# Compression products over columns ordered block by block, with the keys' low parts in two banks of their own

## The chip, the cores and the metric

One Trainium2 chip, one core. The metric is the device time of one execution in microseconds (us); of the runs shown the median is taken. TensorE does the matrix products, VectorE, ScalarE and GpSimd the elementwise work, SyncE issues most transfers.

## What is computed

One step of a decoder layer (D_MODEL 2048) for 256 prompt tokens and 8 samples of 8 tokens, 320 tokens in all. An input projection feeds three attention branches; their outputs are gated, projected, merged and added to the input. The change touches one part of it, the compressed keys and values of the first branch, for the 9 sequences (8 samples with 256 cached rows each, and the prompt):

```python
def compress_tokens(kv, phi_pos, phi_w1, phi_w2):
    # block i covers rows [i*16, i*16 + 32); phi = 2-layer MLP, separate weights for k and v
    sub = kv[:, :n_half * 16].reshape(b, n_half, 16, 2, 2, 128)
    pos = phi_pos.reshape(2, 2, 16, 128)
    w1 = phi_w1.reshape(2, 2, 16, 128, 128)
    for m in range(2):
        part = einsum('bnscgd,csdh->bncgh', sub + pos[:, m], w1[:, m])
        part = part[:, m:m + n_cmp]
        hid = part if hid is None else hid + part
    out = einsum('bncgh,che->bncge', silu(hid), phi_w2)
```

With 256 rows a sequence has 16 half blocks of 16 rows and 15 compressed blocks. Two groups of heads by 9 sequences give 18 row sets, so 288 half blocks, plus two columns for the position embedding.

## The kernel before, in words

**Products.** All weights come as tiles of 2048 x 128, in one stream of 144 tiles that alternate between two buffers u = 0 and 1. A tile is loaded into `raw[u]`, ScalarE rounds it to float32r in `w_hi[u]` (`split_hi`, L536), VectorE puts the rest into `w_lo[u]` (`split_lo`, L814), and TensorE makes three products for each of 16 blocks: high x high, high x low, low x high (`part`, L1327 to L1329), over 320 columns. A split for buffer u waits until TensorE has finished the tile before in it (`mm_done[u]`), and TensorE starts a tile when `lo_ready[u]` says that its low part is there. So while TensorE works on one buffer's tile, the other buffer is split. The next load of a buffer waits for `lo_ready[u]`. The order of the instructions on each engine is written out by hand.

**The compression stage.** At tile pairs J_PHI to J_PHI+3 buffer 0 holds query weights (a `part` of 320 columns) and buffer 1 the compression weights: k = 0, 1 for the keys (c = 0) and k = 2, 3 for the values (c = 1), each with m = 0 (first half of a block) and m = 1 (second half). The raw rows lie in `cmp_t`, by row set q, page g, position s in a half block and half block n within the page (8 per page); the last row set is the position embedding. `cmp_high` (ScalarE, L643) rounds them into `c_hi`, whose row for position s holds 290 columns that count: 16 for each of the 18 row sets and then 2 for the position embedding. `cmp_low` (VectorE, L985) subtracts: for the keys into `c_lo`, in place of the raw rows and in their order, and for the values into `c_lo_pos`, in the order of `c_hi`. The keys are split in two calls by sequences (long before their use), the values in two calls by positions (s below 8, then the rest). The values' high part may overwrite that of the keys only when TensorE has used it: `c_half` comes after the eighth position of k = 1, and the second half waits behind the split of the next weight tile.

For each position TensorE then makes three products (L1450, L1452 or L1454, L1455), all into one bank: S0 and P0 for the keys, S1 and P1 for the values. For the keys the second product reads `c_lo` by a strided pattern of 37 runs of 8 columns, 296 in all; the others read 290 columns in one piece. `pe.wait_ge(c_lo_rdy, ...)` stands before the first position, and for the values before the ninth too.

**Behind it.** `hidden_in` (VectorE, L1000 to L1003) adds the position column of each half and the two halves shifted by one block: four instructions, each of which waits for the one before (`ch.link`). ScalarE's tanh (L658), two more instructions of VectorE (`hidden_out`) and a product with `w_phi2` follow. For the keys this stands in VectorE's order at k = 2, for the values at k = 3. S2 and OB were used last for the rows of the memory values, which ScalarE copies out (L632, `v_rows_rdy`) before the stage; S2 is written again by the product that follows `hidden_out` (L1460).

Of the kernel before, what the change touches and what calls it, by code (L numbers as in the profile page):

```python
# [24 lines left out]
PAGES = PAST // PAGE  # L25
KEYS_S = PAST + DEC_SEQ
SEQS = DEC_BATCH + 1
# [7 lines left out]
NGP = 32  # L35
FIRST_SEQS = 5
HALF = TOK // 2
OUT_PARTS = ((0, 0, 2), (0, 2, 6), (0, 6, 8), (0, 8, 12), (0, 12, 16), (1, 0, 4), (1, 4, 8), (1, 8, 12), (1, 12, 14), (1, 14, 16))
HEAD = ((0, 2), (2, 4), (4, 8), (8, 12), (12, 16))

f32 = mybir.dt.float32
f32r = mybir.dt.float32r
i32 = mybir.dt.int32
ALU = mybir.AluOpType
ACT = mybir.ActivationFunctionType
# [33 lines left out]
def build(nc, A):  # L79
    ctx = ExitStack()  # L80
    with ctx:
# [20 lines left out]
        w_hi = fixed("w_hi", [P, 2, KB, P], f32r)  # L102
        w_lo = fixed("w_lo", [P, 2, KB, P], f32r)
# [15 lines left out]
        st = fixed("st", [P, 16])  # L119
# [21 lines left out]
        cmp_t = at("cmp_t", [P, 2, 2 * SEQS + 1, SEQ], f32, Z_)  # L141
# [132 lines left out]
        def raw_blocks(c, q0, q1, half):  # L274
            return cmp_t[:, c, q0:q1, :].rearrange("p q (g s n) -> p (q g) s n", g=PAGES, s=CMP_STRIDE)[:, :, positions(half), :]

        def by_position(t, q0, q1, half):
            return t[:, positions(half), q0 * CMP_STRIDE:q1 * CMP_STRIDE].rearrange("p s (q n) -> p q s n", n=PAGE // CMP_STRIDE)

        def low_blocks(c, q0, q1, half):  # L280
            if c == 1:
                return by_position(c_lo_pos, q0, q1, half)
            return c_lo[:, q0:q1, :].rearrange("p q (g s n) -> p (q g) s n", g=PAGES, s=CMP_STRIDE)

        def high_blocks(q0, q1, half):
            return by_position(c_hi, q0, q1, half)

        def cross_rows(i, q):

# [241 lines left out]
        def _(act):  # L531
# [106 lines left out]
                for u in range(2):  # L638
                    split_hi(u, k + (J_CMP + 1))

            def cmp_high(c, q0, q1, half=None):
                src, dst = raw_blocks(c, q0, q1, half), high_blocks(q0, q1, half)
                nc.scalar.activation(dst, src, ACT.Copy).then_inc(c_hi_rdy, 1)  # L643

            act.wait_ge(cmp_in, 16 * PAGES * 2 * FIRST_SEQS)
            cmp_high(0, 0, 2 * FIRST_SEQS)
# [5 lines left out]
            cmp_high(0, 2 * FIRST_SEQS, 2 * SEQS + 1)  # L652
            split_hi(0, J_PHI)
            split_hi(1, J_PHI)

# [5 lines left out]
            split_hi(1, J_PHI + 1)  # L661
            split_hi(0, J_PHI + 2)
            act.wait_ge(c_half, 1)
            cmp_high(1, 0, 2 * SEQS + 1, 0)
            split_hi(1, J_PHI + 2)
            cmp_high(1, 0, 2 * SEQS + 1, 1)
            split_hi(0, J_PHI + 3)
            hidden_tanh(0)
            split_hi(1, J_PHI + 3)
# [138 lines left out]
        def _(dve):  # L808
            ch = Chain(dve, dve_chain)
# [122 lines left out]
            v, y, t = st[:, 8:10], st[:, 10:12], st[:, 12:14]  # L932
# [33 lines left out]
            for k in range(2):  # L966
                for u in range(2):
# [3 lines left out]
                    rows = kv_t[:, 2 * k + u, 0:SEQ].rearrange("p (g n s) -> p g s n", g=PAGES, s=CMP_STRIDE)  # L971
# [10 lines left out]
            def cmp_low(c, q0, q1, count, half=None):  # L982
                src, high, dst = raw_blocks(c, q0, q1, half), high_blocks(q0, q1, half), low_blocks(c, q0, q1, half)
                dve.wait_ge(c_hi_rdy, count)
                nc.vector.tensor_tensor(dst, src, high.bitcast(f32), ALU.subtract).then_inc(c_lo_rdy, 1)  # L985

            with dve.Fori(0, J_PHI - J_Q - 2) as k:
                for u in range(2):
                    query_tile(u, k + J_Q, one(q_t, k * 2 + u))
            cmp_low(0, 0, 2 * FIRST_SEQS, 1)  # L990
            for u in range(2):
                query_tile(u, J_PHI - 2, q_t[:, 8 + u, :])
            cmp_low(0, 2 * FIRST_SEQS, 2 * SEQS + 1, 2)
            for u in range(2):
                query_tile(u, J_PHI - 1, q_t[:, 10 + u, :])

            def hidden_in(c):
                first, second = ((S0, P0), (S1, P1))[c]
                rows = hx[:, c, 0:270].rearrange("p (q n) -> p q n", n=N_CMP)
                ch.link(nc.vector.tensor_copy(st[:, c:c + 1], first[:, 288:289]))  # L1000
                ch.link(nc.vector.tensor_scalar_add(rows, first[:, 0:288].rearrange("p (q n) -> p q n", n=CMP_STRIDE)[:, :, 0:N_CMP], st[:, c:c + 1]))
                ch.link(nc.vector.tensor_copy(st[:, c:c + 1], second[:, 289:290]))
                nc.vector.scalar_tensor_tensor(rows, second[:, 0:288].rearrange("p (q n) -> p q n", n=CMP_STRIDE)[:, :, 1:CMP_STRIDE],  # L1003
                                               st[:, c:c + 1], rows, ALU.add, ALU.add).then_inc(hid_x, 1)

            def hidden_out(c):
                dve.wait_ge(hid_e, c + 1)
# [3 lines left out]
            for k in range(4):  # L1011
                query_tile(0, J_PHI + k, q_t[:, 12 + k, :])
                if k == 2:
                    hidden_in(0)
                    hidden_out(0)
                dve.wait_ge(mm_done[1], J_PHI + k + 2)
                dve.sem_inc(w_free[1], 1)
                if k == 1:
                    cmp_low(1, 0, 2 * SEQS + 1, 3, 0)
                if k < 3:  # L1020
                    split_lo(1, J_PHI + k + 1)
                if k == 1:
                    cmp_low(1, 0, 2 * SEQS + 1, 4, 1)
                if k == 3:
                    hidden_in(1)
                    hidden_out(1)
# [232 lines left out]
            v, y, t = st[:, 0:2], st[:, 3:5], st[:, 6:8]  # L1259
# [55 lines left out]
        def _(pe):  # L1315
# [85 lines left out]
            for m, first in enumerate((0, P, TOK - P)):  # L1401
                mm = nc.tensor.matmul(P0[:, m * P:m * P + NGP], v_tmp[:, 0, first:first + P], fold[:], start=True, stop=True)
# [16 lines left out]
            for t in range(4):  # L1419
                u, j = t % 2, J_MEM + 2 + t // 2  # L1420
                pe.wait_ge(lo_ready[u], j + 2)
                for i in range(4):
                    kb = 4 * t + i
                    high, low = (w[:, u, 4 * i:4 * i + 4, :].rearrange("p k c -> p (k c)") for w in (w_hi, w_lo))
                    for n in range(2):
                        out, rows = (S2, OB)[n], slice(n * P, (n + 1) * P)
                        nc.tensor.matmul(out[:], m_hi[:, kb, rows], high, start=(kb == 0), stop=False)  # L1427
                        nc.tensor.matmul(out[:], m_lo[:, kb, rows], high, start=False, stop=False)  # L1428
                        mm = nc.tensor.matmul(out[:], m_hi[:, kb, rows], low, start=False, stop=(kb == KB - 1))  # L1429
# [5 lines left out]
                for u in range(2):  # L1435
                    part(u, k + J_Q, h_hi, h_lo, TOK, ALL)

            used = 2 * SEQS * CMP_STRIDE + CMP_LEN // CMP_STRIDE
            n = PAGE // CMP_STRIDE
            runs = -(-used // n)  # L1440
# [263 lines left out]
            for n, first in enumerate(firsts):  # L1704
                mm = nc.tensor.matmul(S0[:, n:n + 1], y_sum[:, 0, first:first + P], ones[:, 0:1], start=True, stop=True, skip_group_check=True)
# [124 lines left out]
```

## Time and profile before

| | |
|---|---|
| Median of 3 runs | 1113.35 us (1113.16 to 1113.83) |
| Profiled execution, span from first to last instruction | 1110.9 us |
| Median above that span | 2.45 us |
| TensorE busy | 1100.0 us (99%), 8020 products |
| VectorE, ScalarE, GpSimd busy | 606.3, 419.5, 66.8 us |
| Mean granted TensorE clock | 0.996 |

The profiled execution's own time is not listed apart from its span. Products are pipelined: the duration of one reaches beyond the start of the next, so what a product costs is the distance between starts. The third column of a timeline row names the engine, then come the line, the operation, what is written and read, and its shape (partitions x columns); at the end stands how long the engine had been idle and who released it.

### The profile page before, as it was taken

The page shows a single profiled execution, that of the slowest core. Times are in us where ns is not written, and L with a number is a line of the kernel's source. Part 1 is how long each engine was busy: PE and PEld are TensorE (multiplying, and loading weights), DVE is VectorE, ACT ScalarE, POOL GpSimd, SP SyncE. Part 2 cuts the span into 40 slices and gives each one's busy share as a digit, 9 for nine tenths or more (in the row PEclk, how much of TensorE's full clock was granted, in tenths as well). Part 3 has the DMA queues.
Part 4 walks back from the last instruction along what each step waited for, and adds up shares of the span by engine and source line. Part 5 has one row for each costly group of instructions (what it writes and reads, how often), then busy time and mean ns, then how long its engine had stood idle before and what let it go on. Part 6 is the DMA issues. An engine that isn't in the chain of part 4 may idle for free.

```text
span 1110.9 us, 19312 instructions
## 1 busy us (share of the span) xinstructions
PE 1100.0 (99%) x8020; PEld 1077.8 (97%) x8020; DVE 606.3 (55%) x884; ACT 419.5 (38%) x566; POOL 66.8 (6%) x121
## 2 busy tenths in 40 slices
PE   9999999999999999999999999999999999999996
PEld 7998999999999999999999999999999999999996
DVE  6794443536456667664454467455455454454445
ACT  6733322424335444443333344333333333333332
POOL 0014000000000000001100000000000000002220
PEclk9999999999999999999999999999999999999998
DMA  8556685544444232358888744544544444464342
GB/s 297 196 189 201 228 279 189 179 152 152 168 147 173 83 113 110 114 171 295 288 277 306 257 149 171 171 171 171 171 167 153 168 145 144 147 242 146 148 150 95
DMA packets 64081, 202.03 MB, mean 182 GB/s; under 512 B 6647, under 2 KB 35607, under 8 KB 45831
## 3 DMA queue, kind: packets, MB, share of 16 engines
q1 hardware_dynamic: 58888, 185.68, 48.8%
q0 software_dynamic: 2400, 10.89, 2.8%
q10 hardware_dynamic: 2718, 4.41, 1.1%
q8 instruction: 55, 0.90, 0.3%
q14 instruction: 20, 0.16, 0.0%
HBM read 193.61 MB, written 11.53 MB: 185 GB/s over the span
## 4 chain that ended last, share of the span: by engine, by line
PE 99%; DVE 1%; issue 0%; DVEq 0%
PE bank L1327 27%; PE bank L1328 27%; PE bank L1329 27%; PE bank L1679 1%; PE bank L1360 1%; PE bank L1455 1%; PE bank L1450 1%; PE bank L1429 1%; PE bank L1428 1%; PE bank L1427 1%; PE bank L1594 1%; PE bank L1517 0%; PE bank L1452 0%; PE bank L1685 0%; PE bank L1345 0%; PE bank L1454 0%
## 5 line engine op out<-in xcount | busy, mean ns | idle before, releaser
L536 ACT ACTIVATE w_hi<-raw 128x2048 fp32r<-128x2048 f32 x140 | 268.1, 1915 | 572.2 <-PE bank L1329 479.9
L1327 PE MATMUL bank<-h_hi,w_hi 128*128 128x320 f32 x1536 | 479.7, 312 | 0.0
L1329 PE MATMUL bank<-h_hi,w_lo 128*128 128x320 f32 x1536 | 474.6, 309 | 0.0
L1328 PE MATMUL bank<-h_lo,w_hi 128*128 128x320 f32 x1536 | 474.5, 309 | 0.0
L814 DVE TENSOR_TENSOR w_lo<-raw,w_hi 128x2048 fp32r<-128x2048 f32 x140 | 325.2, 2323 | 186.4 <-ACT w_hi L536 186.2
L1327 PEld LDWEIGHTS bank<-h_hi,w_hi 128*128 128x128 f32 x1536 | 288.4, 188 | 3.9 <-issue 3.5
L1328 PEld LDWEIGHTS bank<-h_lo,w_hi 128*128 128x128 f32 x1536 | 288.5, 188 | 0.4
L1329 PEld LDWEIGHTS bank<-h_hi,w_lo 128*128 128x128 f32 x1536 | 288.4, 188 | 0.0
L1328 PE MATMUL bank<-oz_lo,w_hi 128*128 128x320 f32 x256 | 78.9, 308 | 0.0
L1329 PE MATMUL bank<-oz_hi,w_lo 128*128 128x320 f32 x256 | 78.8, 308 | 0.0
L1327 PE MATMUL bank<-oz_hi,w_hi 128*128 128x320 f32 x256 | 78.8, 308 | 0.0
L1327 PE MATMUL bank<-mrg_both,w_hi 128*128 128x320 f32 x224 | 69.0, 308 | 0.0
L1328 PE MATMUL bank<-mrg_both,w_hi 128*128 128x320 f32 x224 | 69.0, 308 | 0.0
L1329 PE MATMUL bank<-mrg_both,w_lo 128*128 128x320 f32 x224 | 69.0, 308 | 0.0
L1201 DVE TENSOR_TENSOR g<-bank,inv 128x320 f32<-128x320 f32 x32 | 15.7, 491 | 72.2 <-PE bank L1329 72.2
L1327 PEld LDWEIGHTS bank<-oz_hi,w_hi 128*128 128x128 f32 x256 | 48.1, 188 | 0.0
L1328 PEld LDWEIGHTS bank<-oz_lo,w_hi 128*128 128x128 f32 x256 | 48.1, 188 | 0.0
L1329 PEld LDWEIGHTS bank<-oz_hi,w_lo 128*128 128x128 f32 x256 | 48.1, 188 | 0.0
L1327 PEld LDWEIGHTS bank<-mrg_both,w_hi 128*128 128x128 f32 x224 | 42.0, 188 | 0.0
L1328 PEld LDWEIGHTS bank<-mrg_both,w_hi 128*128 128x128 f32 x224 | 42.0, 188 | 0.0
L1329 PEld LDWEIGHTS bank<-mrg_both,w_lo 128*128 128x128 f32 x224 | 42.0, 188 | 0.0
L1211 DVE SCALAR_TENSOR_TENSOR bt<-g_t,bank 128x320 f32<-128x320 f32 x16 | 7.8, 487 | 37.8 <-PE bank L1329 37.8
(347 smaller groups left out, 1127.5 us busy)
## 6 DMA issues: line engine op xcount, KB each, us to landing
raw<-in_stream SPq DMA_DIRECT2D x140, 1024.0 KB, 5.0
cmp_t<-in_cmp_pages SPq DMA_DIRECT2D x32, 128.0 KB, 4.2
kt_moba<-in_moba_k SPq DMA_DIRECT2D x16, 256.0 KB, 3.6
kt_mem<-in_mem_k SPq DMA_DIRECT2D x8, 512.0 KB, 6.3
vs_moba<-in_moba_v SPq DMA_DIRECT2D x16, 256.0 KB
vs_mem<-in_mem_v SPq DMA_DIRECT2D x8, 512.0 KB
out_win_old<-in_cache_win POOLq DMA_DIRECT2D x8, 512.0 KB, 3.7
raw<-in_stream SPq DMA_DIRECT2D x10, 256.0 KB, 9.9
```

The costliest lines, as they stand in the source:

```text
L536: nc.scalar.activation(w_hi[:, u], raw[:, u], ACT.Copy).then_inc(hi_ready[u], 1)
L814: nc.vector.tensor_tensor(w_lo[:, u], raw[:, u], w_hi[:, u].bitcast(f32), ALU.subtract).then_inc(lo_ready[u], 1)
L1201: nc.vector.tensor_tensor(g12[:, u, br, :], W[u][:, 0:TOK], inv[:], ALU.mult).then_inc(w_free[u], 1)
L1327: nc.tensor.matmul(out[:, 0:n], w_hi[:, u, kb, :], hi[:, kb, :], start=(kb == first), stop=False)
L1328: nc.tensor.matmul(out[:, 0:n], w_hi[:, u, kb, :], lo[:, kb, :], start=False, stop=False)
L1329: mm = nc.tensor.matmul(out[:, 0:n], w_lo[:, u, kb, :], hi[:, kb, :], start=False, stop=(kb == last))
L1360: mm = nc.tensor.matmul(W[0][:, 0:TOK], raw_a[:, kb, :], x_t[:, kb, :], start=(kb == 0), stop=(kb == KB - 1))
L1427: nc.tensor.matmul(out[:], m_hi[:, kb, rows], high, start=(kb == 0), stop=False)
L1428: nc.tensor.matmul(out[:], m_lo[:, kb, rows], high, start=False, stop=False)
L1429: mm = nc.tensor.matmul(out[:], m_hi[:, kb, rows], low, start=False, stop=(kb == KB - 1))
L1450: nc.tensor.matmul(out[:, 0:used], w_hi[:, 1, s, :], c_hi[:, s, 0:used], start=(s == 0), stop=False, skip_group_check=True)
L1455: mm = nc.tensor.matmul(out[:, 0:used], w_lo[:, 1, s, :], c_hi[:, s, 0:used], start=False, stop=(s == CMP_STRIDE - 1), skip_group_check=True)
```

## The change

The columns of `c_hi` and of `c_lo_pos` are ordered by half block first and row set second: two columns for the position embedding (first half), 16 groups of 18 row sets, two columns for the position embedding again (second half), 292 in all. The first half (m = 0) then needs columns 0 to 271 and the second half columns 20 to 291: 272 each, since the last half block of a row set is not used by the first half, nor the first by the second. ScalarE and VectorE copy and subtract page by page (two instructions in place of one), reading 8 neighbouring half blocks and writing them 18 columns (72 bytes) apart, and do the position columns in small instructions. `c_lo` keeps its order; its products can no longer be added in the same bank, so they go to S2 (m = 0) and OB (m = 1), and `hidden_in` adds those for the keys with four more instructions. TensorE waits once more, for S2 and OB to be copied out, before the stage.

```diff
+CMP_USED = 2 * SEQS * CMP_STRIDE + CMP_LEN // CMP_STRIDE
+CMP_COLS = 2 * SEQS * N_CMP + CMP_LEN // CMP_STRIDE
...
+        def block_columns(t, q0, q1, half, g):
+            columns = t[:, positions(half), 2:2 + CMP_STRIDE * 2 * SEQS].rearrange("p s (g n q) -> p g q s n", g=PAGES, q=2 * SEQS)
+            return columns[:, g, q0:q1]
+
+        def raw_pos(c, half):
+            return cmp_t[:, c, 2 * SEQS, 0:PAGE].rearrange("p (s n) -> p s n", s=CMP_STRIDE)[:, positions(half), 0:2]
+
+        def pos_columns(t, half, m):
+            return t[:, positions(half), m * CMP_USED:m * CMP_USED + 2]
...
-            def cmp_high(c, q0, q1, half=None):
-                src, dst = raw_blocks(c, q0, q1, half), high_blocks(q0, q1, half)
-                nc.scalar.activation(dst, src, ACT.Copy).then_inc(c_hi_rdy, 1)
+            def cmp_high(c, q0, q1, half=None, pos=True):
+                if pos:
+                    for m in range(2):
+                        nc.scalar.activation(pos_columns(c_hi, half, m), raw_pos(c, half), ACT.Copy)
+                nc.scalar.activation(block_columns(c_hi, q0, q1, half, 0), raw_blocks(c, q0, q1, half, 0), ACT.Copy)
+                nc.scalar.activation(block_columns(c_hi, q0, q1, half, 1), raw_blocks(c, q0, q1, half, 1), ACT.Copy).then_inc(c_hi_rdy, 1)
...
+            def cmp_low(c, q0, q1, count, half=None, pos=True):
                 dve.wait_ge(c_hi_rdy, count)
-                nc.vector.tensor_tensor(dst, src, high.bitcast(f32), ALU.subtract).then_inc(c_lo_rdy, 1)
+                if pos:
+                    for m in range(2 if c else 1):
+                        nc.vector.tensor_tensor(low_pos(c, half, m), raw_pos(c, half), pos_columns(c_hi, half, m).bitcast(f32), ALU.subtract)
+                    if c == 0:
+                        rest = [t[:, 2 * SEQS, 0:PAGE].rearrange("p (s n) -> p s n", s=CMP_STRIDE)[:, :, 2:] for t in (c_lo, cmp_t[:, 0])]
+                        nc.vector.tensor_copy(*rest)
+                for g in range(PAGES):
+                    src, high, dst = raw_blocks(c, q0, q1, half, g), block_columns(c_hi, q0, q1, half, g), low_blocks(c, q0, q1, half, g)
+                    ins = nc.vector.tensor_tensor(dst, src, high.bitcast(f32), ALU.subtract)
+                ins.then_inc(c_lo_rdy, 1)
...
-                ch.link(nc.vector.tensor_copy(st[:, c:c + 1], first[:, 288:289]))
...
+                ch.link(nc.vector.tensor_copy(st[:, c:c + 1], first[:, 0:1]))
+                ch.link(nc.vector.tensor_scalar_add(rows, by_row(first, 2), st[:, c:c + 1]))
+                ch.link(nc.vector.tensor_copy(st[:, c:c + 1], second[:, 271:272]))
+                ins = nc.vector.scalar_tensor_tensor(rows, by_row(second, 0), st[:, c:c + 1], rows, ALU.add, ALU.add)
+                if c == 0:
+                    for m, low in enumerate((S2, OB)):
+                        ch.link(ins)
+                        ch.link(nc.vector.tensor_copy(st[:, c:c + 1], low[:, 288 + m:289 + m]))
+                        blocks = low[:, 0:288].rearrange("p (q n) -> p q n", n=CMP_STRIDE)[:, :, m:m + N_CMP]
+                        ins = nc.vector.scalar_tensor_tensor(rows, blocks, st[:, c:c + 1], rows, ALU.add, ALU.add)
...
+            pe.wait_ge(v_rows_rdy, 2 + 4)
...
+                columns = slice(0, CMP_COLS) if m == 0 else slice(2 * SEQS + 2, 2 * SEQS + 2 + CMP_COLS)
...
-                    nc.tensor.matmul(out[:, 0:used], w_hi[:, 1, s, :], c_hi[:, s, 0:used], start=(s == 0), stop=False, skip_group_check=True)
+                    nc.tensor.matmul(out[:, 0:CMP_COLS], w_hi[:, 1, s, :], c_hi[:, s, columns], start=(s == 0), stop=False)
                     if c == 0:
-                        nc.tensor.matmul(out[:, 0:runs * n].rearrange("p (q n) -> p q n", n=n), w_hi[:, 1, s, :], low[:, s, 0:runs], start=False, stop=False, skip_group_check=True)
+                        nc.tensor.matmul((S2, OB)[m][:, 0:runs * n].rearrange("p (q n) -> p q n", n=n), w_hi[:, 1, s, :], low[:, s, 0:runs],
+                                         start=(s == 0), stop=(s == CMP_STRIDE - 1))
                     else:
-                        nc.tensor.matmul(out[:, 0:used], w_hi[:, 1, s, :], c_lo_pos[:, s, 0:used], start=False, stop=False, skip_group_check=True)
-                    mm = nc.tensor.matmul(out[:, 0:used], w_lo[:, 1, s, :], c_hi[:, s, 0:used], start=False, stop=(s == CMP_STRIDE - 1), skip_group_check=True)
+                        nc.tensor.matmul(out[:, 0:CMP_COLS], w_hi[:, 1, s, :], c_lo_pos[:, s, columns], start=False, stop=False)
+                    mm = nc.tensor.matmul(out[:, 0:CMP_COLS], w_lo[:, 1, s, :], c_hi[:, s, columns], start=False, stop=(s == CMP_STRIDE - 1))
```

## Rows read from the trace of the kernel before

**Rows 1.** The chain that ended last: shares of the span by engine.

```profile
PE 99%; DVE 1%; issue 0%; DVEq 0%
```

**Rows 2.** Waits of TensorE: total us, times, longest us.

```profile
PE bank L1345 <- DVE ones L822: 1.7, 1, 1.7
PE bank L1693 <- DVE y_diag L1274: 1.6, 1, 1.6
PE bank L1717 <- DVE y_last L1257: 0.7, 1, 0.7
```

**Rows 3.** Compression products by form; busy times by engine, then granted clock (1.00), DMA.

```profile
L1455 PE MATMUL bank<-c_hi,w_lo 128*128 128x290 f32 x64 | 19.2, 299 | 0.0
L1450 PE MATMUL bank<-c_hi,w_hi 128*128 128x290 f32 x64 | 19.0, 297 | 0.0
L1452 PE MATMUL bank<-c_lo,w_hi 128*128 128x296 f32 x32 | 10.3, 323 | 0.0
L1454 PE MATMUL bank<-c_lo_pos,w_hi 128*128 128x290 f32 x32 | 9.5, 298 | 0.0
...
274.30:280.70 6.40, 6.40 (x50) 6.40 (x49) 2.78 (x2) 1.92 (x1) 0.00 (x0) 1.00 0.46 127
```

**Rows 4.** Timeline of TensorE, first products of tiles: start us, us, engine, line.

```profile
225.99 0.31 PE L1327 MATMUL bank<-h_hi,w_hi 128*128 128x320 f32 x1
...
233.03 0.30 PE L1450 MATMUL bank<-c_hi,w_hi 128*128 128x290 f32 x1
...
239.92 0.31 PE L1327 MATMUL bank<-h_hi,w_hi 128*128 128x320 f32 x1
...
260.87 0.29 PE L1450 MATMUL bank<-c_hi,w_hi 128*128 128x290 f32 x1
...
274.35 0.29 PE L1450 MATMUL bank<-c_hi,w_hi 128*128 128x290 f32 x1
...
280.80 0.62 PE L1460 MATMUL bank<-hid,w_phi 128*128 128x270 f32 x2
```

**Rows 5.** Timeline of TensorE in the memory stage: 256 columns, then 512.

```profile
69.95 0.28 PE L1327 MATMUL bank<-m_hi,w_hi 128*128 128x256 f32 x1
...
91.38 0.39 PE L1427 MATMUL bank<-w_hi,m_hi 128*128 128x512 f32 x1
...
102.13 0.39 PE L1429 MATMUL bank<-w_lo,m_hi 128*128 128x512 f32 x1
102.36 0.39 PE L1427 MATMUL bank<-w_hi,m_hi 128*128 128x512 f32 x1
```

**Rows 6.** Timeline of VectorE around the compression.

```profile
202.27 2.83 DVE L985 TENSOR_TENSOR c_lo<-cmp_t,c_hi 128x2560 fp32r<-128x2560 f32 x1
...
217.41 2.56 DVE L985 TENSOR_TENSOR c_lo<-cmp_t,c_hi 128x2304 fp32r<-128x2304 f32 x1 [1.00 <-ACT c_hi L643]
...
254.15 2.69 DVE L985 TENSOR_TENSOR c_lo_pos<-cmp_t,c_hi 128x2432 fp32r<-128x2432 f32 x1 [2.69 <-PE bank L1455]
...
258.95 2.68 DVE L985 TENSOR_TENSOR c_lo_pos<-cmp_t,c_hi 128x2432 fp32r<-128x2432 f32 x1
...
266.00 0.16 DVE L1002 COPY st<-bank 128x1 f32<-128x1 f32 x1
266.20 0.50 DVE L1003 SCALAR_TENSOR_TENSOR hx<-bank,st,hx 128x270 f32<-128x270 f32 x1
...
269.52 2.29 DVE L814 TENSOR_TENSOR w_lo<-raw,w_hi 128x2048 fp32r<-128x2048 f32 x1 [1.55 <-ACT w_hi L536]
```

**Rows 7.** Timeline of ScalarE around the compression.

```profile
250.57 2.25 ACT L643 ACTIVATE c_hi<-cmp_t 128x2432 fp32r<-128x2432 f32 x1 [1.45 <-PE bank L1455]
...
266.74 0.43 ACT L658 ACTIVATE he<-hx 128x270 f32<-128x270 f32 x1 [3.69 <-DVE hx L1003]
267.58 1.92 ACT L536 ACTIVATE w_hi<-raw 128x2048 fp32r<-128x2048 f32 x1 [0.41 <-PE bank L1455]
```

**Rows 8.** VectorE's copy of the prompt's rows (L972): ns min/median/max, first and last start.

```profile
L972 DVE COPY cmp_t<-kv_t x4: 392/400/403, 121.2 to 142.3; 128x256 f32<-128x256 f32 x4
```

More of the change, by code:

```diff
@@ L272, in positions, with raw_blocks, low_blocks, low_pos @@
             return slice(0, CMP_STRIDE) if half is None else slice(half * CMP_STRIDE // 2, (half + 1) * CMP_STRIDE // 2)
[L274 to L280, printed above, removed]
-            if c == 1:
[L282 to L286, printed above, removed]
+        def raw_blocks(c, q0, q1, half, g):
+            return cmp_t[:, c, q0:q1, :].rearrange("p q (g s n) -> p g q s n", g=PAGES, s=CMP_STRIDE)[:, g, :, positions(half), :]
+        def block_columns(t, q0, q1, half, g):
[5 more added lines that the diff above has]
+            return t[:, positions(half), m * CMP_USED:m * CMP_USED + 2]
+        def low_blocks(c, q0, q1, half, g):
+            if c == 1:
+                return block_columns(c_lo_pos, q0, q1, half, g)
+            return c_lo[:, q0:q1, :].rearrange("p q (g s n) -> p g q s n", g=PAGES, s=CMP_STRIDE)[:, g]
+        def low_pos(c, half, m):
+            if c == 1:
+                return pos_columns(c_lo_pos, half, m)
+            return c_lo[:, 2 * SEQS, 0:PAGE].rearrange("p (s n) -> p s n", s=CMP_STRIDE)[:, :, 0:2]
         def cross_rows(i, q):
@@ L639, in _ @@
                     split_hi(u, k + (J_CMP + 1))
-            def cmp_high(c, q0, q1, half=None):
-                src, dst = raw_blocks(c, q0, q1, half), high_blocks(q0, q1, half)
-                nc.scalar.activation(dst, src, ACT.Copy).then_inc(c_hi_rdy, 1)
+            def cmp_high(c, q0, q1, half=None, pos=True):
[4 more added lines that the diff above has]
+                nc.scalar.activation(block_columns(c_hi, q0, q1, half, 1), raw_blocks(c, q0, q1, half, 1), ACT.Copy).then_inc(c_hi_rdy, 1)
             act.wait_ge(cmp_in, 16 * PAGES * 2 * FIRST_SEQS)
-            cmp_high(0, 0, 2 * FIRST_SEQS)
+            cmp_high(0, 0, 2 * FIRST_SEQS, pos=False)
             for u in range(2):
@@ L651, in _ @@
             act.wait_ge(pos_in, 16)
-            cmp_high(0, 2 * FIRST_SEQS, 2 * SEQS + 1)
+            cmp_high(0, 2 * FIRST_SEQS, 2 * SEQS)
             split_hi(0, J_PHI)
@@ L663, in _ @@
             act.wait_ge(c_half, 1)
-            cmp_high(1, 0, 2 * SEQS + 1, 0)
+            cmp_high(1, 0, 2 * SEQS, 0)
             split_hi(1, J_PHI + 2)
-            cmp_high(1, 0, 2 * SEQS + 1, 1)
+            cmp_high(1, 0, 2 * SEQS, 1)
             split_hi(0, J_PHI + 3)
@@ L980, in query_tile @@
                 split_lo(u, j + 1)
-            def cmp_low(c, q0, q1, count, half=None):
-                src, high, dst = raw_blocks(c, q0, q1, half), high_blocks(q0, q1, half), low_blocks(c, q0, q1, half)
+            def cmp_low(c, q0, q1, count, half=None, pos=True):
                 dve.wait_ge(c_hi_rdy, count)
-                nc.vector.tensor_tensor(dst, src, high.bitcast(f32), ALU.subtract).then_inc(c_lo_rdy, 1)
+                if pos:
[8 more added lines that the diff above has]
+                ins.then_inc(c_lo_rdy, 1)
             with dve.Fori(0, J_PHI - J_Q - 2) as k:
@@ L989, in _ @@
                     query_tile(u, k + J_Q, one(q_t, k * 2 + u))
-            cmp_low(0, 0, 2 * FIRST_SEQS, 1)
+            cmp_low(0, 0, 2 * FIRST_SEQS, 1, pos=False)
             for u in range(2):
                 query_tile(u, J_PHI - 2, q_t[:, 8 + u, :])
-            cmp_low(0, 2 * FIRST_SEQS, 2 * SEQS + 1, 2)
+            cmp_low(0, 2 * FIRST_SEQS, 2 * SEQS, 2)
             for u in range(2):
@@ L999, in hidden_in, with by_row @@
                 rows = hx[:, c, 0:270].rearrange("p (q n) -> p q n", n=N_CMP)
-                ch.link(nc.vector.tensor_copy(st[:, c:c + 1], first[:, 288:289]))
[L1001 to L1004, printed above, removed]
+                def by_row(bk, first):
+                    return bk[:, first:first + 270].rearrange("p (n q) -> p q n", q=2 * SEQS)
+                ch.link(nc.vector.tensor_copy(st[:, c:c + 1], first[:, 0:1]))
[8 more added lines that the diff above has]
+                        ins = nc.vector.scalar_tensor_tensor(rows, blocks, st[:, c:c + 1], rows, ALU.add, ALU.add)
+                ins.then_inc(hid_x, 1)
             def hidden_out(c):
@@ L1018, in _ @@
                 if k == 1:
-                    cmp_low(1, 0, 2 * SEQS + 1, 3, 0)
+                    cmp_low(1, 0, 2 * SEQS, 3, 0)
                 if k < 3:
@@ L1022, in _ @@
                 if k == 1:
-                    cmp_low(1, 0, 2 * SEQS + 1, 4, 1)
+                    cmp_low(1, 0, 2 * SEQS, 4, 1)
                 if k == 3:
@@ L1436, in _ @@
                     part(u, k + J_Q, h_hi, h_lo, TOK, ALL)
-            used = 2 * SEQS * CMP_STRIDE + CMP_LEN // CMP_STRIDE
             n = PAGE // CMP_STRIDE
-            runs = -(-used // n)
+            runs = -(-CMP_USED // n)
+            pe.wait_ge(v_rows_rdy, 2 + 4)
             low = c_lo[:].rearrange("p q (g s n) -> p s (q g) n", g=PAGES, s=CMP_STRIDE)
```

## The prediction

> **What bounds the kernel now.** I read the chain of waits first. It lies on TensorE for 99% of the span [rows 1], so only what TensorE does or waits for can move the time. Next, who TensorE waited for: three waits, 4.0 us together, one on the first instruction and two in the final normalization [rows 2]. Between them it never stood still for another engine, so a product that becomes shorter makes the end earlier by as much, and work added to VectorE or ScalarE costs nothing until it makes a TensorE tile late.
>
> Then the products that the diff touches [rows 3]: 64 + 64 + 32 = 160 of 290 columns, and 32 of 296 columns (low parts of the keys). The durations there (297 to 323 ns) are no price: they overlap. The price is the distance from start to start, read in the timeline.
> - 320 columns: 48 products from 225.99 to 233.03, 7.04 us, 146.7 ns each [rows 4].
> - 290 columns: the last compression tile, 48 products from 274.35 to 280.80, 6.45 us, 134.4 ns each [rows 4].
> - Tile with the strided low product: 233.03 to 239.92, 6.89 us [rows 4]. It is 0.44 us longer than the one above for the same number of products, so each of its 16 products of 296 columns costs about 27 ns more than a product of 290.
> - 256 columns: the product at 69.95 is the fourth of 192, so 189 of them reach to 91.38: 113.4 ns each [rows 5].
> - 512 columns: 48 products from 91.38 to 102.36, 228.8 ns each [rows 5].
>
> The granted clock is 1.00 of 2.4 GHz there [rows 3], so streaming alone would take 133.3, 120.8, 106.7 and 213.3 ns for 320, 290, 256 and 512 columns. What lies above streaming is 13.4, 13.6, 6.7 and 15.5 ns.
>
> **The change, part by part.**
> 1. *160 products go from 290 to 272 columns.* No row shows 272. From the 290 row, with the slope between 290 and 320 (12.3 ns over 30 columns, 0.41 ns a column), it is 134.4 - 18 x 0.41 = 127.0 ns: 7.4 ns less, times 160 is 1.18 us. The line between 256 and 290 (0.62 ns a column) gives 123.3 ns, 1.8 us in all. If 272 carried only the 6.7 ns above streaming that 256 does, it would be 120.0 ns, 2.3 us in all. I take 1.2 us, since three of four widths carry 13 to 16 ns above streaming and 272 lies above 256; 2.3 us stays as the far end.
> 2. *Second halves read from column 20* (80 bytes into a row) instead of column 0: 80 of the 160 products. No row isolates a start offset. The nearest is the strided low product, 27 ns dearer; its short runs are a far stronger disturbance than one offset. The bounds are 0 and 80 x 27 ns = 2.2 us; I take 0, since the stream itself stays contiguous.
> 3. *Low parts of the keys into two other banks.* The 32 products keep their 296 columns and their strided read, so their price stays. TensorE now changes banks before and after each. The nearest rows are the value products of the memory, which change bank after every third: from the last product in one bank (102.13) to the first in the other (102.36) is 0.23 us, the mean of all of them [rows 5]. I take 0. The extra 27 ns might also vanish with the shared bank: 32 x 27 = 0.9 us, the bound on the gain's side. The one added wait, for the memory rows to have left those banks, stands on copies that ScalarE makes before the queries' tiles even begin: 0.
> 4. *ScalarE's splits.* Each of the four high-part instructions becomes two, and three of the four calls get two tiny ones for the position columns. Elements go from 2432 to 2304 + 32 for the value halves. Between 270 elements in 0.43 us and 2432 in 2.25 us lie 0.84 ns an element and 0.20 us of fixed time [rows 7], so three more instructions less 96 elements make +0.5 us per call. The high part of the first value half ends at 252.82; VectorE takes it up at 254.15 [rows 6, 7]. Hidden by 1.3 us, by 0.8 us after the addition.
> 5. *VectorE's splits.* A tiny copy takes 0.16 us [rows 6]. A value half gets two tiny instructions and the fixed time of one more, and loses 96 elements (0.1 us): +0.4 us at most. The binding point is the second value half: it runs from 258.95 for 2.68 us, to 261.63 [rows 6], and TensorE wants it 24 products into its tile, at 260.87 + 24 x 0.134 = 264.1 [rows 4]. Margin 2.5 us, less 24 x 7.4 ns because the tile now runs faster, less 0.8 us for both halves: 1.5 us remain. Cost 0. The key splits are further from their use.
> 6. *The key sum gets four more instructions* in a chain where each waits for the one before: two copies (0.16 us) and two additions over 270 columns (0.50 us), with 0.04 us between [rows 6]: +1.5 us. ScalarE's tanh, which started at 266.74 and took 0.43 us [rows 7], waits for that; queued behind it on ScalarE is the weight split that started at 267.58 and fed VectorE's at 269.52 [rows 6, 7]. Now the tanh ends at 268.7, the weight split (1.9 us) at 270.6, and VectorE's (2.29 us) at 272.9. TensorE wants it when its next 320-column tile ends, at 274.35 [rows 4], 0.36 us earlier after the shorter tile: 274.0. Margin 1.1 us: cost 0, though this is the thinnest cover. The value sum has no added instruction.
> 7. *Reads and writes with a step of 72 bytes* in the ScalarE and VectorE splits, and from the sum's banks. What the trace has is a VectorE copy with a step of 64 bytes on its reading side: 256 elements in 400 ns [rows 8], about 1.04 ns an element after some 0.13 us of fixed time. The present low-part subtraction runs at that rate too (2.69 us for 2432 elements, [rows 6]). So a long step on a read did not go below one element a cycle. No row has a long step on a write. Bounds: 0, or twice the time per element. I take 0.
>
> The Trainium skill ("SBUF — State Buffer", section "Door 1: The DMA port swizzle") speaks against part 7: it says that memory is served in lines of 16 bytes, and that each access that crosses to a new line pays. By it the splits would slow down and the sum would be that of the slower rival below. The copy in the trace does not bear it out for reads by VectorE.
>
> **Sum:** -1.18 us, nothing added. The profiled execution's span goes from 1110.9 to 1109.7 us; the median of 1113.35 us lies 2.45 us above that span, taken as unchanged, and goes to 1112.2; I say 1112.1.
>
> **The rivals.**
> - *Cheaper spacing* (chance 0.18). Products of 272 behave like those of 256, or the low products lose their extra cost. The times are 1113.35 - 2.3 = 1111.05, or 1113.35 - 1.2 - 0.9 = 1111.25, both together 1110.15. For it: the 256 rows do have the smaller excess. Against it: 290, 320 and 512 agree on the larger one, and the strided read stays.
> - *The gain is not kept* (chance 0.10). The offset of part 2, or the bank changes, take 5 to 15 ns from a product here and there: between 1112.6 and 1114.3, most likely about 1113.3. Against it: no row shows such a loss for a contiguous stream.
> - *Slower: long steps double the time per element* (chance 0.07). VectorE first: its two value halves take 5.2 us each. The first ends at 259.35, the weight split behind it at 261.6 instead of before 260.87 (0.7 us of standstill), the second half at 266.8 where TensorE is at 264.65 (2.15 us), and the late key sum adds 0.3 us to the next tile. That is 3.2 - 1.2 = +2.0 us, 1115.35. If ScalarE's writes double too (2.2 us more per call), the value halves start 0.75 us later, and the key splits that began on VectorE at 202.27 and 217.41 [rows 6] push the weight splits behind them past TensorE's tile starts by 1.0 and 1.7 us: 1118.8. It decides from where the second half's margin is used up: 1.5 us over 4608 elements, 0.33 ns each, about 1.3 times the present time per element.
> - Main case, chance 0.65.
>
> **How the numbers follow.** A measurement of this kernel can tell about 0.2%, 2.2 us, from no change. The main case (1.2 us) lies inside, and so does "not kept". Of the cheaper-spacing rival about 0.14 passes 2.2 us. The slower rival is counted whole (0.07), though its milder form comes out just inside, and 0.01 is added for other losses. Faster 0.14, same 0.78, slower 0.08. The range reaches down to 1110.8 (cheaper spacing without both effects together) and up to 1113.9 (most of "not kept"); outside are the slower rival and the two extremes.
>
> **What would show it.** Right: spacing of about 127 ns in the value tiles, so 6.1 us for 48 products instead of 6.45; 6.65 us instead of 6.89 in the key tiles; still no wait of TensorE between the first and the last stage; splits of ScalarE and VectorE at 0.83 and 1.04 ns an element. Wrong: 5.8 us for a value tile (cheaper spacing); a TensorE wait on the low parts of the values or on a weight split near 260 or 274 us (slower rival, or the thin cover of part 6); second-half tiles longer than first-half tiles (the offset).

## The result and the profile after

The change made the kernel slower: 1118.76 us median (1118.10 to 1121.70, 5 runs) against 1113.18 us (1112.59 to 1113.83) beside it, a ratio of 1.0056 (95% interval 1.0045 to 1.0067). The forecast was 1112.1 us, in a range from 1110.8 to 1113.9, with 0.08 for slower. Of the experiments' executions two ran at a mean granted clock of 0.85 and 0.87 (1193.6 us for the narrower products alone, 1179.0 us for the step in the keys' splits alone); they count in no ratio, and without them the two medians given below as 1111.84 and 1116.59 us would be 1111.70 and 1116.53 us.

The page of the changed kernel, its first line and the chain of waits by engine, where [rows 1] had 99% on TensorE:

```profile
span 1119.9 us, 19336 instructions
...
PE 94%; DVE 3%; ACT 1%; DMA 1%; issue 0%; SPq 0%; DVEq 0%; ACTq 0%
```

VectorE, ScalarE and a transfer are now on the chain. The waits of TensorE (total us, times, longest) have three lines that [rows 2] did not have:

```profile
PE bank L1359 <- DVE w_lo L828: 3.5, 2, 2.8
...
PE bank L1483 <- DVE w_lo L828: 1.4, 1, 1.4
PE bank L1483 <- DVE c_lo_pos L1006: 1.2, 1, 1.2
```

TensorE's timeline shows where they are: the last product ahead of each standstill and the first two behind it.

```profile
212.47 0.31 PE L1361 MATMUL bank<-h_hi,w_lo 128*128 128x320 f32 x1
213.45 0.41 PE L1359 MATMUL bank<-h_hi,w_hi 128*128 128x320 f32 x1 [0.67 <-DVE w_lo L828]
213.70 0.30 PE L1360 MATMUL bank<-h_lo,w_hi 128*128 128x320 f32 x1
...
227.48 0.31 PE L1361 MATMUL bank<-h_hi,w_lo 128*128 128x320 f32 x1
230.58 0.61 PE L1359 MATMUL bank<-h_hi,w_hi 128*128 128x320 f32 x1 [2.79 <-DVE w_lo L828]
230.99 0.47 PE L1360 MATMUL bank<-h_lo,w_hi 128*128 128x320 f32 x1
...
267.47 0.31 PE L1361 MATMUL bank<-h_hi,w_lo 128*128 128x320 f32 x1
269.19 0.39 PE L1483 MATMUL bank<-c_hi,w_hi 128*128 128x272 f32 x1 [1.41 <-DVE w_lo L828]
269.42 0.28 PE L1488 MATMUL bank<-c_lo_pos,w_hi 128*128 128x272 f32 x1
...
272.19 0.29 PE L1489 MATMUL bank<-c_hi,w_lo 128*128 128x272 f32 x1
273.71 0.39 PE L1483 MATMUL bank<-c_hi,w_hi 128*128 128x272 f32 x1 [1.23 <-DVE c_lo_pos L1006]
273.94 0.28 PE L1488 MATMUL bank<-c_lo_pos,w_hi 128*128 128x272 f32 x1
```

From the first to the third row of each group, less the distances that the two products would have had anyway (147 ns for 320 columns, 125 ns for 272, 267 ns for 320 at half clock), the standstills cost 0.94, 3.10, 1.68 and 1.50 us, 7.2 us together: two before query tiles behind the keys' splits, two in the first value tile. The granted clock (the column behind the POOL busy time) fell to half, 1.2 GHz, shortly before the second one ended, and stayed there behind it, in this execution:

```profile
228.00:230.00 2.00, 0.00 (x0) 0.00 (x0) 2.00 (x2) 1.79 (x1) 0.00 (x0) 0.94 0.00 0
230.00:232.00 2.00, 1.42 (x5) 1.45 (x6) 2.00 (x3) 0.00 (x0) 0.00 (x0) 0.50 0.18 25
232.00:234.00 2.00, 2.00 (x9) 2.00 (x9) 1.08 (x1) 0.00 (x0) 0.00 (x0) 0.50 0.86 356
...
236.00:238.00 2.00, 2.00 (x13) 2.00 (x13) 0.00 (x0) 0.00 (x0) 0.00 (x0) 0.86 0.69 291
```

In it 22 products of 320 columns started 267 ns apart instead of 147: 2.6 us. The last value tile gives the other side, the gain:

```profile
283.87 0.29 PE L1483 MATMUL bank<-c_hi,w_hi 128*128 128x272 f32 x1
...
289.86 0.62 PE L1494 MATMUL bank<-hid,w_phi 128*128 128x270 f32 x2
```

48 products in 5.99 us, 124.8 ns each, where [rows 4] had 134.4. For 160 products that is 1.5 us. The account of this execution: 7.2 + 2.6 - 1.5 = +8.3 us in the stage, against +9.0 us in the span; the stage began some 0.7 us later too. This was the longest of the five executions (mean clock 0.994; the two shortest, at 0.997, took 1118.1 and 1118.2 us).

Why VectorE was late, in its own timeline, against [rows 6] (a row that ends in x2 is two instructions one after the other, with their common time):

```profile
205.67 5.05 DVE L1006 TENSOR_TENSOR c_lo<-cmp_t,c_hi 128x1280 fp32r<-128x1280 f32 x2 [2.63 <-ACT c_hi L657]
...
223.85 4.03 DVE L1006 TENSOR_TENSOR c_lo<-cmp_t,c_hi 128x1024 fp32r<-128x1024 f32 x2
...
262.36 4.58 DVE L1006 TENSOR_TENSOR c_lo_pos<-cmp_t,c_hi 128x1152 fp32r<-128x1152 f32 x2
...
269.19 4.46 DVE L1006 TENSOR_TENSOR c_lo_pos<-cmp_t,c_hi 128x1152 fp32r<-128x1152 f32 x2
```

The subtractions of a value half now take 4.5 us for 2304 elements, where 2432 had taken 2.69. ScalarE's copies grew alike: two of 1152 elements in 2.33 and 2.35 us, where one of 2432 had taken 2.25 [rows 7].

### The profile page after: what moved, and what is told of

It is laid out like the page before. It is cut to its first block, busy times and chain, and to the rows that moved or that the text cites. A ratio compares the mean times of both kernels' runs of the same rounds, so it can differ in the third digit from the quotient of the medians.

```text
span 1119.9 us, 19336 instructions
## 1 busy us (share of the span) xinstructions
PE 1102.5 (98%) x8020; PEld 1079.1 (96%) x8020; DVE 615.2 (55%) x898; ACT 428.5 (38%) x576; POOL 66.4 (6%) x121
## 4 chain that ended last, share of the span: by engine, by line
PE 94%; DVE 3%; ACT 1%; DMA 1%; issue 0%; SPq 0%; DVEq 0%; ACTq 0%
PE bank L1359 26%; PE bank L1361 26%; PE bank L1360 26%; PE bank L1713 1%; DVE c_lo L1006 1%; DVE c_lo_pos L1006 1%; PE bank L1392 1%; PE bank L1461 1%; PE bank L1460 1%; PE bank L1459 1%; ACT c_hi L657 1%; DVE w_lo L828 1%; DMA x_t<-in_x_t 1%; PE bank L1628 1%; PE bank L1483 1%; PE bank L1489 1%
```

## The experiments

**Is it the step, or the number of instructions?** The rival to the step was the additional instructions and the longer key sum. The edit puts the 8 half blocks of a page next to each other again and leaves everything else as in the change:

```diff
-            columns = ...rearrange("p s (g n q) -> p g q s n", g=PAGES, q=2 * SEQS)
+            columns = ...rearrange("p s (g q n) -> p g q s n", g=PAGES, q=2 * SEQS)
```

> The changed kernel with one thing undone: in the rows of c_hi and c_lo_pos the 8 half blocks of a row set stand next to each other again (step 4 bytes instead of 72); the number of instructions, elements, products and columns is that of the change. It leaves out the right assignment of columns to blocks. Theory 'long steps double the time per element': the halves of the values' splits go back to about 1.15 us on ScalarE and 1.35 us on VectorE, no wait of TensorE in the stage, 1113.2 - 1.5 = 1111.7 us. Rival 'two instructions and the position columns make the engines late': they stay long, about 1118.8 us.

Measured: 1111.74 us against 1113.37 (0.9986, 0.9976 to 0.9995). No wait of TensorE in the stage is left. Two groups, busy us and mean ns, of this run:

```profile
L1006 DVE TENSOR_TENSOR c_lo_pos<-cmp_t,c_hi 128x1152 fp32r<-128x1152 f32 x4 | 5.2, 1352 | 0.0
...
L656 ACT ACTIVATE c_hi<-cmp_t 128x1152 fp32r<-128x1152 f32 x2 | 2.5, 1227 | 0.0
```

The step alone makes the difference between 1111.7 and 1118.8 us. The additional instructions and the longer sum cost nothing that can be measured: the next run has neither and takes 1111.84 us.

**What are the narrower products worth?**

```diff
-    nc.tensor.matmul(out[:, 0:used], w_hi[:, 1, s, :], c_hi[:, s, 0:used], ...)
+    nc.tensor.matmul(out[:, 0:272], w_hi[:, 1, s, :], c_hi[:, s, cols], ...)   # cols = 0:272 or 20:292, three products
```

> The kernel before, with only the 160 products at 272 columns (first halves from column 0, second halves from column 20), the splits and the sum as before. It leaves out columns that the sum needs. What the narrower products are worth alone: the trace of the changed kernel has 125.0 ns from start to start for 272 columns against 134.4 for 290, so 160 x 9.4 = 1.5 us: 1111.7 us. Rival, that part of the gain in the key tiles (0.35 and 0.28 us there) comes from the banks: less than 1.5 us, about 1.3.

Measured: 1111.84 us (0.9986, 0.9976 to 0.9996), 1.5 us less. The first key tile, with all three products in one bank:

```profile
234.30 0.29 PE L1451 MATMUL bank<-c_hi,w_hi 128*128 128x272 f32 x1
...
240.84 0.31 PE L1327 MATMUL bank<-h_hi,w_hi 128*128 128x320 f32 x1
```

It takes 6.54 us. In the changed kernel, with banks of their own for the low parts, the same tile takes 6.54 us too:

```profile
240.40 0.29 PE L1483 MATMUL bank<-c_hi,w_hi 128*128 128x272 f32 x1
...
246.94 0.31 PE L1359 MATMUL bank<-h_hi,w_hi 128*128 128x320 f32 x1
```

The second key tile takes 6.60 us in both. So the banks neither cost nor save anything, and the low product keeps what it costs above the others. The gain in the key tiles is smaller because only two of their three products got narrower.

**What does a step cost by itself?** Subtractions and copies behind the last work, for example with 18 elements:

```diff
+    ch.link(nc.vector.tensor_tensor(fl[:, 2304:3456].rearrange("p (n q) -> p q n", q=18), <contiguous>, <contiguous>, ALU.subtract))
+    ach.link(nc.scalar.activation(fa[:, 2304:3456].rearrange("p (n q) -> p q n", q=18), <contiguous>, ACT.Copy))
```

> The kernel before with 20 instructions of 1152 elements added behind its last work, on memory nobody uses any more: VectorE subtractions and ScalarE copies, in which the written or the read operand has a step of 1, 2, 4, 8 or 18 elements. Theory 'each step beyond some size costs on every operand': contiguous 1.35 us (VectorE) and 1.16 us (ScalarE), with a written step of 18 about 2.35 and 2.3 us, with a read step of 18 the same. Rival 'only writes pay': a read step leaves 1.35 and 1.16 us. Rival 'it is contention between the two engines and the transfers in that stage, not the step': all of them near 1.35 and 1.16 us here, where the chip is quiet.

Lines of that run (ns, smallest, median, largest of one). VectorE: contiguous, written step 2, 4, 18, read step 18; ScalarE: contiguous, written step 2, 4, 18, read step 18:

```profile
L1328 DVE TENSOR_TENSOR raw<-raw x1: 1348/1348/1348, 1107.6 to 1107.6; 128x1152 f32<-128x1152 f32 x1
L1329 DVE TENSOR_TENSOR raw<-raw x1: 1359/1359/1359, 1109.0 to 1109.0; 128x1152 f32<-128x1152 f32 x1
L1330 DVE TENSOR_TENSOR raw<-raw x1: 2201/2201/2201, 1110.4 to 1110.4; 128x1152 f32<-128x1152 f32 x1
...
L1332 DVE TENSOR_TENSOR raw<-raw x1: 2320/2320/2320, 1114.9 to 1114.9; 128x1152 f32<-128x1152 f32 x1
...
L1336 DVE TENSOR_TENSOR raw<-raw x1: 2314/2314/2314, 1123.1 to 1123.1; 128x1152 f32<-128x1152 f32 x1
L809 ACT ACTIVATE raw<-raw x1: 1162/1162/1162, 1127.9 to 1127.9; 128x1152 f32<-128x1152 f32 x1
L810 ACT ACTIVATE raw<-raw x1: 1231/1231/1231, 1129.1 to 1129.1; 128x1152 f32<-128x1152 f32 x1
L811 ACT ACTIVATE raw<-raw x1: 2223/2223/2223, 1130.3 to 1130.3; 128x1152 f32<-128x1152 f32 x1
...
L813 ACT ACTIVATE raw<-raw x1: 2362/2362/2362, 1134.9 to 1134.9; 128x1152 f32<-128x1152 f32 x1
...
L817 ACT ACTIVATE raw<-raw x1: 2362/2362/2362, 1143.1 to 1143.1; 128x1152 f32<-128x1152 f32 x1
```

A step of 8 bytes is nearly free; one of 16 bytes and more adds 0.74 to 0.84 ns an element to VectorE's subtraction and 0.9 to 1.0 to ScalarE's copy. It makes no difference whether it stands on the reading or on the writing side, and a second operand with a step adds nothing (written and read with a step of 18: 2321 ns). No other engine works there, and the transfer engines' busy share is 0.12 during VectorE's instructions and 0.00 during ScalarE's, so contention is not the cause: that rival falls, and so does "only writes pay".

**Why did the copy of [rows 8] look free?**

```diff
+    ch.link(nc.vector.tensor_copy(fl[:, 2304:2560].rearrange("p (q n) -> p q n", q=16), fl[:, 0:256].rearrange("p (n q) -> p q n", q=16)))
```

> The kernel before with more VectorE instructions behind its last work: copies of 1152 elements with a read step of 1, 2, 3, 4, 16, 18 and a written step of 2, 3, 18; subtractions with a step of 3 and 6; additions of 504 elements from a bank with a step of 1, 2, 18; the copy of 256 elements with a step of 1 and 16. It asks why the copy in rows 8 looked free of charge. Theory: a contiguous copy runs at two elements a cycle (about 0.75 us for 1152), so that its 1.04 ns an element with a long step was already the slow form: the 256 elements take about 0.27 us contiguous and 0.4 us with a step of 16. Rival: a copy's reads are free, contiguous 0.4 us too. Step 3 (12 bytes) lies between steps 2 and 4 if each touched line of 16 bytes costs. Reads from a bank cost nothing for a step (the sum's instructions took 0.50 us in both kernels).

Copies of 1152 elements contiguous and with a step of 4; additions of 504 elements from a bank, contiguous and with a step of 18; the copy of 256 elements contiguous and with a step of 16:

```profile
L1314 DVE COPY raw<-raw x1: 750/750/750, 1108.0 to 1108.0; 128x1152 f32<-128x1152 f32 x1
...
L1317 DVE COPY raw<-raw x1: 1185/1185/1185, 1111.3 to 1111.3; 128x1152 f32<-128x1152 f32 x1
...
L1327 DVE TENSOR_SCALAR raw<-bank,ones x1: 741/741/741, 1126.7 to 1126.7; 128x504 f32<-128x504 f32 x1
...
L1329 DVE TENSOR_SCALAR raw<-bank,ones x1: 744/744/744, 1128.2 to 1128.2; 128x504 f32<-128x504 f32 x1
L1330 DVE COPY raw<-raw x1: 294/294/294, 1129.0 to 1129.0; 128x256 f32<-128x256 f32 x1
L1331 DVE COPY raw<-raw x1: 375/375/375, 1129.3 to 1129.3; 128x256 f32<-128x256 f32 x1
```

A contiguous copy runs at 0.51 ns an element ((750 - 294) / 896 elements), twice as fast as a subtraction. The copy of the kernel before was already slowed by its step; it only looked like full speed beside instructions of another kind. Reads from a bank pay nothing for a step of 8 or 72 bytes. For the subtraction a step of 12 bytes lies between (written with a step of 3 it took 1701 ns). For VectorE's copy two things do not follow the pattern of the subtraction. A step of 16 bytes and more adds less, 0.33 to 0.43 ns an element (1130 to 1243 ns with steps of 4, 16 and 18, in place of 750). And a step of 3 costs more than one of 4: 1680 ns read and 1670 written. Why is open.

**Can the step be moved to the raw rows?** The loop order inside the splits is turned, so that the row sets run innermost (for `c_lo` too; the indices are turned with it):

```diff
-    raw:     "p q (g s n) -> p g q s n"      columns: "p s (g n q) -> p g q s n"
+    raw:     "p q (g s n) -> p g s n q"      columns: "p s (g n q) -> p g s n q"
```

> The change with the order inside the split instructions turned: the row sets run innermost, so that c_hi and c_lo_pos are written and read in one piece, and the raw rows are read (for the keys also written back) with a step of 1024 bytes. Same result as the change. If only writes pay for a long step: ScalarE's splits and the values' low parts run at 0.83 and 1.04 ns an element, only the keys' low parts stay slow; about 1112 to 1114 us. If reads pay too: about 1118.8 us, as the change.

Measured: 1119.78 us (1.0054, 1.0037 to 1.0070), no better than the change. One operand with a long step is enough. In the profiled execution a value half takes 4.4 to 4.5 us on VectorE, as in the change.

**Keys and values apart.** `block_columns` takes the neighbouring order for one of the two:

```diff
+            order = "p s (g n q) -> p g q s n" if c == 0 else "p s (g q n) -> p g q s n"   # keys; c == 1 for values
```

> The changed kernel, with the 72-byte step kept in the keys' splits alone; the values' splits write and read neighbouring columns. It leaves out the right assignment of columns to blocks for the values. In the trace of the changed kernel TensorE stood still for 0.97 and 3.07 us before two query tiles behind the keys' splits, and then ran 22 products at half clock (266.7 ns in place of 146.7, 2.6 us). Theory 'a standstill of 3 us costs twice, once as waiting and once as clock': 1111.7 + 4.0 + 2.6 = 1118.4 us, with a stretch at 0.50 granted clock behind the second standstill. Rival 'the clock fell by accident in that one profiled execution': 1115.8 us and full clock.

> The changed kernel, with the 72-byte step kept in the values' splits alone; the keys' splits are as in the run that put the half blocks next to each other. It leaves out the right assignment of columns to blocks for the keys. Theory: only the two standstills of the value tile remain (1.7 and 1.5 us), each below 2 us, and the clock stays full: 1111.7 + 3.2 = 1114.9 us. Rival 'the two parts delay each other' (one late split makes the next one later): clearly less than 3.2 us above 1111.7.

Measured: keys 1116.59 us (1.0028, 1.0018 to 1.0038), values 1114.92 us (1.0015, 1.0006 to 1.0023). The values' part came out as expected, 3.2 us above 1111.74, at full clock. The keys' part is 4.9 us, between the two expectations. The clock did fall at the 3 us standstill in the profiled execution, but for a shorter time: 10 products at half clock, 1.2 us, instead of 22.

```profile
230.00:232.00 2.00, 1.92 (x7) 1.95 (x8) 2.00 (x2) 0.00 (x0) 0.00 (x0) 0.50 0.45 90
232.00:234.00 2.00, 2.00 (x13) 2.00 (x12) 0.58 (x1) 0.00 (x0) 0.00 (x0) 0.76 0.97 406
```

Two executions of this kernel had a mean clock of 0.997 and took 1115.0 and 1116.0 us, the others 0.995 or 0.996 and took 1116.3 to 1117.0 us. The profiled execution of the run before this one had a standstill of 2.7 us in the same place and 11 products at half clock behind it. So the profiled executions show a loss by the clock of 1.2 to 2.6 us. That some had none is read from their mean clocks and times alone, since no trace of such an execution was kept; it would explain most of the 3.6 us between the change's own runs (0.997 up to 1118.8 us, 0.995 at 1120.2, 0.994 at 1121.7).

**Why 3 us and not 1.7?** The slower rival had priced the second key standstill at 1.7 us. SyncE's timeline of the changed kernel has the last cache pages here, and then ScalarE's first instruction behind them:

```profile
213.34 0.34 SPq L326 DMA_DIRECT2D raw<-in_stream  x1
214.43 1.28 SPq L344 DMA_DIRECT2D cmp_t<-in_cmp_pages  x2
```

```profile
219.36 0.35 ACT L655 ACTIVATE c_hi<-cmp_t 128x32 fp32r<-128x32 f32 x2 [4.58 <-DMA cmp_t<-in_cmp_pages]
```

In the kernel before, the same pages were issued some 4 us earlier:

```profile
210.48 1.28 SPq L333 DMA_DIRECT2D cmp_t<-in_cmp_pages  x2
```

They stand behind a weight load that waits for the weight split (`lo_ready`), and in the changed kernel that split stood behind the slow key split and ended at 213.32, when the load was issued:

```profile
211.02 2.30 DVE L828 TENSOR_TENSOR w_lo<-raw,w_hi 128x2048 fp32r<-128x2048 f32 x1
```

The edit issues the pages two weight loads earlier:

```diff
+            for b, n in order[:2]:
+                compression_page(b, n)
             for k, (b, n) in enumerate(order):
+                if k + 2 < len(order):
+                    compression_page(*order[k + 2])
                 weight_tile(n, J_CMP + 1 + b)
```

> The run with the long step in the keys' splits alone (1116.6 us), with one thing more: SyncE issues the last cache pages two weight loads earlier, so that they no longer stand behind the load that waits for the late weight split. In the changed kernel the last page transfer was issued at 214.43 instead of 210.48 and ScalarE waited for it until 219.36 before the second key split. Theory 'the first standstill delays the pages, and the pages make the second standstill 3 us long': with the pages in time ScalarE starts the second key split 4 us earlier, the second standstill falls from 3.1 us to at most 1.7 us, the clock stays full, and the time is 1113 to 1114.4 us. Rival 'the second standstill comes from the slow splits alone': it stays at 3.1 us, with the clock's loss behind it, 1116.6 us.

Measured: 1112.65 us (0.9993, 0.9984 to 1.0002), although the keys' splits were as slow as in the change. ScalarE's timeline now has no wait ahead of the second key split, and VectorE's part of it is as long as it was (4.03 us in the change):

```profile
215.82 0.34 ACT L659 ACTIVATE c_hi<-cmp_t 128x32 fp32r<-128x32 f32 x2
```

```profile
220.35 4.06 DVE L1010 TENSOR_TENSOR c_lo<-cmp_t,c_hi 128x1024 fp32r<-128x1024 f32 x2
```

Only the first standstill is left; the second did not shrink but went away, and with it the clock's loss. So the second slow key split by itself cost nothing; its 3.1 us came from the late pages. Between the two runs that is 3.9 us, standstill and clock together; in the changed kernel it was 3.1 us and, where the clock fell, up to 2.6 more. It came through a transfer that nobody had touched.

**A version that keeps the gain.** Only half block 0 and half block 15 of a row set have to stand apart from the others. The columns are ordered: position columns, half block 0 of all row sets, half blocks 1 to 14 of each row set next to each other, half block 15 of all row sets, position columns. Both halves still need 272 columns.

```diff
+        def edge_columns(t, q0, q1, half, m):
+            return t[:, positions(half), 2 + 270 * m + q0:2 + 270 * m + q1]
...
-            columns = t[:, positions(half), 2:2 + CMP_STRIDE * 2 * SEQS].rearrange("p s (g n q) -> p g q s n", ...)
+            columns = t[:, positions(half), 20:272].rearrange("p s (q g n) -> p g q s n", g=PAGES, q=2 * SEQS)
```

> Same result as the change, other column order: position columns, half block 0 of all row sets, then the half blocks 1 to 14 of a row set next to each other, then half block 15 of all row sets, position columns. Both halves again need 272 columns, but the bulk of the splits runs in pieces of 7 neighbours; only the two edge blocks (288 elements in a value half) have a long step on the reading side. Expected: per value half VectorE 2 x 1.2 + 2 x 0.45 + 0.3 = 3.5 us in place of 4.8, ScalarE 2 x 1.05 + 2 x 0.4 + 0.3 = 3.2 us; within the margins, so the products' gain is kept: 1111.8 us. If the cover of the key sum (now two small instructions longer) is gone: up to 1 us more, 1112.8 us.

Measured: 1112.07 us (1110.92 to 1112.38, 11 runs) against 1113.14 (0.9987, 0.9978 to 0.9996): faster than the kernel before by 1.1 us and than the change by 6.7. VectorE's first value half, edges and bulk:

```profile
254.09 0.76 DVE L1018 TENSOR_TENSOR c_lo_pos<-cmp_t,c_hi 128x144 fp32r<-128x144 f32 x2
254.76 2.31 DVE L1021 TENSOR_TENSOR c_lo_pos<-cmp_t,c_hi 128x1008 fp32r<-128x1008 f32 x2
```

With the position columns ahead of them (0.26 us) it takes 3.2 us, and TensorE waits for nothing in the stage. Runs of 7 neighbours (28 bytes) cost no more than runs of 8: 1008 elements in 1.16 us here, 1152 in 1.35 before. Shorter runs were not tried.

## Why the prediction was wrong, point by point

1. **Narrower products** (predicted 127.0 ns and 1.2 us): right, the size a little short. Measured were 125 ns and 1.5 us, about halfway between the slope that was taken and the line between 256 and 290 columns (123.3 ns), which stood as an alternative.
2. **Start at column 20** (0 taken): right. In the run with the narrower products alone the first and second halves take 6.54 and 6.60 us for the keys, 6.05 and 5.99 us for the values: no loss from the offset.
3. **Banks of their own** (0 taken): right; the same 6.54 us with shared banks. The low products did not get cheaper either.
4. and 5. **More instructions on ScalarE and VectorE**: right as far as their number goes (1111.74 us with all of them and no step). The margins hold only at the old rate.
6. **The key sum with four more instructions**, the thinnest cover: it held, in every run, and even with two small ones more in the last version. Reading the banks with a step cost nothing.
7. **This is the step that failed: "Bounds: 0, or twice the time per element. I take 0."** The upper bound was the truth: 1.9 ns an element on VectorE instead of 1.04. The reading behind it was that the copy of [rows 8] "did not go below one element a cycle". But a contiguous copy takes 0.51 ns an element, half of that, so that row showed the slowdown and not its absence. It should have been compared with a copy of its own kind without a step. Even that comparison (294 against 375 ns) would have shown only that there is a price, and not its size for a subtraction, which is about twice as large per element; a bound from another operation is none. Four waits of TensorE, 7.2 us in the profiled execution, stand where the prediction had 0. That memory is served in lines of 16 bytes, as the Trainium skill says ("SBUF — State Buffer", section "Door 1: The DMA port swizzle"), fits the subtractions and ScalarE's copies: a step of 8 bytes is free, and the full price is there from 16 bytes on. VectorE's copy with a step of 12 bytes (1680 ns, against 1185 with 16) does not fit it. I had let one misread row outweigh it.

The slower rival, at 0.07, had the mechanism, the long steps, and its time of 1118.8 us is the measured one to 0.1 us; in that there is luck. It had 3.9 us in the value part and the tile behind it, where 3.2 were measured: the last 0.3 us did not arise, a value half took 4.6 us on VectorE instead of 5.2, and ScalarE's delay was 1.1 us instead of 0.75. In the keys' part it had 1.0 and 1.7 us (measured 0.9 and 3.1), nothing for the clock (up to 2.6), and 1.2 us of gain (1.5). Its 1.7 us had the wrong cause too: it took them for the price of the slow split itself, which was nothing once the pages came in time. It did not follow the late weight split on to SyncE's queue, where the next load waits for it and the cache pages stand behind that load. The prediction's part on the keys' splits said only that they were further from their use, and looked at no queue but TensorE's.

## What to carry to other kernels

An order of columns that shortens TensorE's products is paid by whoever writes that order: keep runs of neighbours (7 were enough here), and put apart only the columns that have to be. Take the price of an access pattern from two instructions of the same kind that differ in the pattern alone. Where an engine with slack gets slower, follow every semaphore it raises into the transfer queues: a load that waits holds up all transfers behind it, also those of another tensor.

## What was not expected of the hardware

- A step of 16 to 72 bytes on any one operand in memory adds 0.74 to 0.84 ns an element to a VectorE subtraction and 0.9 to 1.0 to a ScalarE copy, equally for reads and writes; to a VectorE copy it adds 0.33 to 0.43. A step of 8 bytes adds under 0.1 ns in all three. One of 12 bytes adds 0.3 ns to the subtraction and 0.8 to the VectorE copy. VectorE's reads from a bank do not show it.
- A standstill of TensorE of about 3 us can cost a second time: in all three profiled executions that had one (2.7 to 3.1 us) the clock fell to 1.2 GHz before it ended, for 3.4 to 6.8 us in all, and 10 to 22 products ran at it. The mean clocks suggest that other executions of the same kernels were spared. The standstills of up to 1.7 us were followed by no fall of the clock.
